# Hybrid decoder block on eight cores: norm factors in PSUM banks, a six-bank rotation and three changes to the planner's due times

## The chip, the cores and the metric

The kernel runs on the 8 cores of one Trainium2 chip as one program. Each core works on its own 2048 tokens (two sequences of 8192, four cores each) and nothing is exchanged between cores. The metric is the device time of one execution in microseconds, which is that of the slowest core. The profile is taken on the slowest core of one execution.

## The reference

```
for l in range(DEPTH):                                   # DEPTH = 1
    mod = (silu(c) @ w_ada[l] + b_ada[l])[:, None, :]
    sh1, sc1, ga1, sh2, sc2, ga2 = split(mod, 6)
    h = rms_norm(x, g_mix[l]) * (1 + sc1) + sh1
    z = h @ w_in[l] + b_in[l]
    q, k, v, conv_b, conv_c, conv_x, gate_a, gate_c = split(z, ...)
    attn = sliding_window_sink_attention(q, k, v, sinks[l])      # window 128
    conv = conv_b * causal_depthwise_conv(conv_c * conv_x, conv_w[l])   # 3 taps
    merged = sigmoid(gate_a) * attn + sigmoid(gate_c) * conv
    x = x + ga1 * (merged @ w_out[l])
    h = rms_norm(x, g_ffn[l]) * (1 + sc2) + sh2
    g_part, u_part = split(h @ w_ffn_in[l], 2)
    x = x + ga2 * ((silu(g_part) * u_part) @ w_ffn_out[l])
return rms_norm(x, g_final)
```

Width 1024, 16 query heads and 2 key heads of 64, feed-forward width 2816. All arrays are float32 in memory; the kernel multiplies in bfloat16.

## The kernel before

A core keeps its tokens in four tiles of 512, channels on the partitions. X (`xres`, float32) holds the residual, H (`h`, bfloat16) the normed input of either sub-layer, MG (`mg`) the merged branches and later the feed-forward activations.

Each operation is recorded with its engine, the intervals that it reads and writes, a cost in us, a priority and perhaps a `lat`. A planner (`schedule`, a list scheduler) then simulates the five engines with these costs: of the operations that are ready on an engine it takes the one with the lowest priority number, and an operation is ready when each of its inputs is done, plus `lat`. What it finds is a fixed order for each engine's queue. On the chip the engines follow these orders and wait only on semaphores. `lat` and the priorities thus put no wait into the program: they only place an instruction further back in its queue. `step_pos` counts the priority up by one for each piece of work.

The stages, in order:

1. Start and mixing (0 to about 510 us). Token-major tiles are squared and scaled (`prep`), turned by TensorE and evicted with shift and scale into H (`turned`, `turn`, L531 to L543). Then eight chunks of channels run: query, gate, convolution groups (`group`, L593), attention in nine steps (L721 to L773) and the merge on GpSimd (L784). The groups take PSUM banks 0 to 3 in rotation (`nb`), the scores banks 4 and 5, the attention sums banks 6 and 7. Between chunks 1 and 3, `mods_rows` makes the four late modulation vectors: a weight of 4 MB comes in over the GpSimd queue (`wadaB`), 16 matmuls in two halves (L791) give partial sums, ScalarE copies them out (L796), SyncE writes them to memory and reads them back transposed (L799, L802), and VectorE adds them up (L806, L809).
2. Output projection and the first feed-forward groups (about 504 to 605 us). `w_out` does eight groups of eight matmuls for each tile (L911), VectorE evicts them into X (L917), ScalarE squares (L896, L901) and GpSimd adds the squares into ACC (L903). `second_norm` follows for each tile: `rstd_of` sums ACC over partitions with one matmul (L470), ScalarE takes the root into RS (L473), VectorE the reciprocal into RS (L475), then eight products X times factor into H (L928, VectorE) and eight scale-and-shift instructions (L933, ScalarE). The tiles come in the order w0, w1, w2, f0, w3, f1, f2, f3, where f is the first four feed-forward steps (`ff_in`: two groups at L968, silu at L973, product at L976).
3. The rest of the feed-forward (605 to about 1036 us): three groups of hidden chunks, `ff_in` and `ff_out` (L981, evicted at L988).
4. `finish_tile`: the last norm in the same way, the products at L1004 on VectorE or L1009 on GpSimd, and the output transfers.

From stage 2 on, `nb` rotates over eight banks, in the order 4, 5, 6, 7, 0, 1, 2, 3, and `rstd_of` takes its bank from the same rotation. The bank of a group is fixed by the order in which the program records the groups. The bank of tile 2's sum (its root is the last reader) is therefore also that of the last group of f0.

Of the kernel before, what the change touches and what calls it, by code (L numbers as in the profile page):

```python
# [289 lines left out]
def build_program():  # L290
# [87 lines left out]
    with es:  # L378
# [86 lines left out]
        P.op("act", lambda e: e.activation(out=ESINK.t[:], in_=cst(O_SINK, 8), func=AF.Exp), reads=[cst_iv], writes=[ESINK.iv()], cost=1.5)  # L465


        def rstd_of(total, n, sd, slack=1.5):
            b = nb()
            P.op("pe", [lambda e: e.matmul(bank(b)[:, 0:n], lhsT=ONESF.t[:], rhs=total[0][total[1], total[1] + n], start=True, stop=True)],  # L470
                 reads=[ONESF.iv(), total[0].iv(total[1], total[1] + n)], writes=[pv_(b)], cost=4 * n / 2400 + 0.2, lat=slack)
            d, o = sd
            P.op("act", lambda e: e.activation(out=d[o, o + n], in_=bank(b)[:, 0:n], func=AF.Sqrt, bias=EPSC.t[:], scale=1.0 / D),  # L473
                 reads=[pv_(b), EPSC.iv()], writes=[d.iv(o, o + n)], cost=act_us(n))
            P.op("dve", lambda e: e.reciprocal(out=d[o + n, o + 2 * n], in_=d[o, o + n]),  # L475
                 reads=[d.iv(o, o + n)], writes=[d.iv(o + n, o + 2 * n)], cost=0.1 + n * 0.0066)

        def scaled(src, a, n, rs, hcol, eng):
            d, o = rs
            P.op(eng, lambda e: e.tensor_tensor(out=h3[:, :, hcol:hcol + n], in0=src[a, a + 8 * n].rearrange("p (k t) -> p k t", k=8),  # L480
                                                in1=d[o, o + n].rearrange("p (o t) -> p o t", o=1).to_broadcast([128, 8, n]), op=ALU.mult),
                 reads=[src.iv(a, a + 8 * n), d.iv(o, o + n)], writes=h_iv(hcol, n),
                 cost=dve_us(8 * n) if eng == "dve" else pool_us(8 * n))

        def affine(hcol, n, acol, shcol, ivs):
            for k in range(8):
                P.op("dve", lambda e, k=k: e.tensor_scalar(out=hk(k, hcol, n), in0=hk(k, hcol, n), scalar1=acol[:, k:k + 1],
                                                           scalar2=shcol[:, k:k + 1], op0=ALU.mult, op1=ALU.add),
                     reads=ivs + [H.iv(k * NTH + hcol, k * NTH + hcol + n)], writes=[H.iv(k * NTH + hcol, k * NTH + hcol + n)],
                     cost=dve_us(n, 4))  # L490


        def stats(src, a, nblk, s0, out, engs=("act",)):
# [56 lines left out]
            scale(X, tt * 4096, 4, 1 + 4 * tt, XN, ("dve",) * 4 if tt == 1 else ("dve", "act", "dve", "dve"))  # L550

        def turned(tt):
            turn(XN, 4, 128 + 512 * tt, None, ("dve",))

        stats(X, 0, 4, 1, XN0)
        stats(XH, 0, 1, 0, XNH)
# [231 lines left out]
        def mods_rows(slot, v):  # L788
            for hf in range(2):
                b = nb()  # L790
                P.op("pe", [lambda e, i=i, q=q, b=b, hf=hf: e.matmul(bank(b)[32 * q:32 * q + 32, :], lhsT=SCREP[(4 * i + q) * 32, (4 * i + q + 1) * 32],  # L791
                                                         rhs=WA[1][(4 * i + q) * 1024 + hf * 512, (4 * i + q) * 1024 + hf * 512 + 512],
                                                         start=(i == 0), stop=(i == 1), skip_group_check=True, tile_position=(0, 32 * q))
                            for i in range(2) for q in range(4)],
                     reads=[WA[1].iv(), SCREP.iv()], writes=[pv_(b)], cost=0.8)
                P.op("act", lambda e, hf=hf, b=b: e.activation(out=MROW[hf * 512, hf * 512 + 512], in_=bank(b), func=AF.Copy),  # L796
                     reads=[pv_(b)], writes=[MROW.iv(hf * 512, hf * 512 + 512)], cost=act_us(512, 0))
            dv = ("d", slot, slot + 1)
            P.op("sp", lambda e: e.dma_start(out=mscr_d[slot], in_=MROW.t[0:128:32, :]), reads=[MROW.iv()], writes=[dv],  # L799
                 dma="d_mr", cost=0.1, nbytes=16384)  # L800
            mo = slot * 32
            P.op("sp", lambda e: e.dma_start(out=MC4[mo, mo + 32].rearrange("p (q j) -> p q j", q=4),  # L802
                                             in_=mscr_d[slot].rearrange("q (j p) -> p q j", p=128),
                                             allow_slow_non_contiguous=True),
                 reads=[dv], writes=[MC4.iv(mo, mo + 32)], dma="d_mc", cost=0.1, nbytes=600000)
            P.op("dve", lambda e: e.tensor_reduce(out=MODC[v * 8, v * 8 + 8], in_=MC4[mo, mo + 32].rearrange("p (q j) -> p j q", q=4),  # L806
                                                  axis=AX.X, op=ALU.add),
                 reads=[MC4.iv(mo, mo + 32)], writes=[MODC.iv(v * 8, v * 8 + 8)], cost=0.2)
            P.op("dve", lambda e: e.tensor_tensor(out=MODC[v * 8, v * 8 + 8], in0=MODC[v * 8, v * 8 + 8], in1=cst(O_BADA + 8 * v, 8), op=ALU.add),  # L809
                 reads=[MODC.iv(v * 8, v * 8 + 8), cst_iv], writes=[MODC.iv(v * 8, v * 8 + 8)], cost=0.2)  # L810
            if v == 4:
                P.op("dve", lambda e: e.scalar_tensor_tensor(out=A2.t[:], in0=MODC[32, 40], scalar=1.0, in1=cst(O_GFFN, 8),
                                                             op0=ALU.add, op1=ALU.mult),
                     reads=[MODC.iv(32, 40), cst_iv], writes=[A2.iv()], cost=0.2)
# [106 lines left out]

        def second_norm(tt):
            ro = (tt % 2) * 1024
            rstd_of((ACC, (tt % 2) * 512), 512, (RS, ro))
            P.prio = pos[0] + 9
            for k in range(8):
                a = tt * 4096 + k * 512
                P.op("dve", lambda e, a=a, k=k: e.tensor_tensor(out=hk(k, 128 + 512 * tt, 512), in0=X[a, a + 512], in1=RS[ro + 512, ro + 1024], op=ALU.mult),  # L928
                     reads=[X.iv(a, a + 512), RS.iv(ro + 512, ro + 1024)], writes=[H.iv(k * NTH + 128 + 512 * tt, k * NTH + 640 + 512 * tt)],
                     cost=dve_us(512))  # L930
            for k in range(8):
                iv = H.iv(k * NTH + 128 + 512 * tt, k * NTH + 640 + 512 * tt)
                P.op("act", lambda e, k=k: e.activation(out=hk(k, 128 + 512 * tt, 512), in_=hk(k, 128 + 512 * tt, 512), func=AF.Identity,  # L933
# [258 lines left out]
```

How the kernel before makes its waits and increments, by code:

```python
    def replay(self, eng, engine, sems):  # L245
        for o in self.order[eng]:
            for s, v in self.waits[o.idx].items():
                engine.wait_ge(sems[s], v)
            ins = None
            for fn in o.fns:
                ins = fn(engine)
            if o.dma is not None:
                ins.then_inc(sems[o.dma], 16)
            elif o.need:
                ins.then_inc(sems[eng], 1)
# [847 lines left out]
        @block.sync  # L1103
        def _(eng):
            P.replay("sp", eng, sems)
            for i in range(8):
                eng.wait_ge(sems[f"d_o{i}"], P.dma_cnt[f"d_o{i}"])
```

## Time and profile before

| | us |
|---|---|
| median of 3 runs | 1089.92 |
| lowest and highest of them | 1057.12, 1121.12 |
| the profiled execution | 1056.61 |
| its span, slowest core (core 0) | 1054.5 |
| fastest core (core 3) | 1040.8 |
| TensorE busy on core 0 | 961.6 (91%) |
| VectorE busy | 585.1 (55%) |
| ScalarE, GpSimd busy | 385.6, 209.1 |

The execution's own time is 2.11 us above the span of its slowest core. A busy share says how long an engine had an instruction in it, not that it bounds the stage. Line numbers such as L968 are those of the kernel before; PE is TensorE, PEld its weight load, DVE VectorE, ACT ScalarE, POOL GpSimd, SP SyncE.

### The profile page before, as it was taken

The numbers are of one execution on the slowest core, as the hardware profiler recorded it, in microseconds if no ns is written. First come the engines' busy times: TensorE is split into PE (matmuls) and PEld (weight loads), VectorE is DVE, ScalarE is ACT, GpSimd is POOL, SyncE is SP. The second block draws the span as 40 slices with busy tenths as digits, with TensorE's granted clock in tenths as the row PEclk, the third lists the DMA queues.
The fourth block names the chain that finished last, engine by engine and source line by source line (L and its number), as shares of the span: only waits on it lengthen the run. The fifth ranks groups of instructions, "written<-read, shape, count | busy, mean of one in ns | idle before, by whom it ended". The sixth has DMA issues, their size and how long they took to land.

```text
span 1054.5 us, 15358 instructions; the slowest of 8 cores (1040.8 to 1054.5 us)
## 1 busy us (share of the span) xinstructions
PE 961.6 (91%) x5474; PEld 452.4 (43%) x5571; DVE 585.1 (55%) x829; ACT 385.6 (37%) x592; POOL 209.1 (20%) x282
## 2 busy tenths in 40 slices
PE   0469999999979999999998999999999999999993
PEld 0335444444434444444443444444444444444443
DVE  1247858586857877878868531234212244253656
ACT  4166545454535454545266531100111100233233
POOL 2100222222211212121563410000100001023213
PEclk9989999999989999999998999999999999999997
DMA  9970462855244434032800432210522202110222
GB/s 191 226 175 1 60 111 29 125 96 81 48 53 128 91 130 91 11 56 36 136 16 11 71 57 44 40 21 1 91 40 40 40 1 47 23 66 15 80 80 81
DMA packets 44651, 72.26 MB, mean 69 GB/s; under 512 B 19600, under 2 KB 21904, under 8 KB 42528
## 3 DMA queue, kind: packets, MB, share of 16 engines
q0 software_dynamic: 21600, 45.36, 27.1%
q1 hardware_dynamic: 22976, 25.91, 8.1%
q8 instruction: 46, 0.75, 0.3%
q14 instruction: 29, 0.24, 0.1%
HBM read 108.15 MB, written 8.45 MB: 111 GB/s over the span
## 4 chain that ended last, share of the span: by engine, by line
PE 78%; DVE 8%; DMA 6%; issue 4%; ACT 2%; POOL 1%; DVEq 0%; ACTq 0%; POOLq 0%; SPq 0%
PE psum L968 28%; PE psum L593 27%; PE psum L981 14%; DMA wadaB<-w_ada_l 5%; PE psum L911 3%; PE psum L745 3%; DVE rden L770 2%; PE psum L721 2%; DMA mc<-mscr 1%; DVE h L928 1%; DVE h L543 1%; DVE cv L668 1%; DVE nrm L771 1%; DVE pT L733 1%; PE psum L531 0%
## 5 line engine op out<-in xcount | busy, mean ns | idle before, releaser
L593 PE MATMUL psum<-h,ws 128*128 128x512 bf16 (+1 forms) x1694 | 366.0, 366 | 15.7 <-issue 5.7
L968 PE MATMUL psum<-h,fws 128*128 128x512 bf16 x1380 | 306.1, 380 | 6.0 <-ACT rs L473 4.5
L593 PEld LDWEIGHTS psum<-h,ws 128*128 128x128 bf16 x1744 | 161.4, 99 | 188.6 <-issue 38.6
L968 PEld LDWEIGHTS psum<-h,fws 128*128 128x128 bf16 x1408 | 138.0, 98 | 173.3 <-issue 9.4
L976 DVE TENSOR_TENSOR mg<-psum,sg 128x512 bf16<-128x512 f32 x88 | 60.4, 688 | 196.5 <-PE psum L968 189.6
L973 ACT ACTIVATE sg<-psum 128x512 bf16<-128x512 f32 x88 | 52.1, 596 | 307.6 <-PE psum L968 297.6
L981 PE MATMUL psum<-mg,fwo 128*128 128x512 bf16 (+1 forms) x747 | 152.4, 363 | 1.7 <-DVE mg L976 1.0
L770 DVE RECIPROCAL rden<-rden 128x256 f32<-128x256 f32 x64 | 111.9, 1749 | 12.6 <-ACT rden L768 11.6
L988 DVE SCALAR_TENSOR_TENSOR xres<-psum,modc,xres 128x512 f32<-128x512 f32 (+1 forms) x104 | 73.7, 709 | 78.3 <-PE psum L981 77.5
L981 PEld LDWEIGHTS psum<-mg,fwo 128*128 128x128 bf16 x760 | 74.3, 98 | 79.2 <-issue 1.5
L784 POOL TENSOR_TENSOR mg<-nrm,cv 128x256 bf16<-128x256 f32 x64 | 53.8, 840 | 273.8 <-DVE cv L690 141.4
L903 POOL TENSOR_TENSOR acc<-acc,sq 128x512 f32<-128x512 f32 (+1 forms) x58 | 69.7, 1203 | 126.0 <-ACT sq L901 120.6
L730 ACT ACTIVATE pT<-psum 128x1024 bf16<-128x1024 f32 (+2 forms) x72 | 66.7, 926 | 52.8 <-PE psum L721 52.8
L911 PE MATMUL psum<-mg,ws 128*128 128x512 bf16 x250 | 57.5, 383 | 3.5 <-ACT rs L473 1.3
L955 POOL DMA_DIRECT2D fws<-w_fi_l x44 | 23.5, 536 | 170.3 <-PE psum L968 155.7
L733 DVE TENSOR_TENSOR pT<-pT,mask 128x1024 bf16<-128x1024 bf16 (+2 forms) x72 | 45.8, 640 | 12.1 <-ACT pT L730 11.5
L668 DVE SCALAR_TENSOR_TENSOR cv<-u,cst,cv 128x512 f32<-128x512 f32 x64 | 48.0, 749 | 7.6 <-ACT cv L665 4.9
L901 ACT ACTIVATE sq<-xres 128x512 f32<-128x512 f32 (+1 forms) x63 | 36.2, 581 | 41.9 <-DVE xres L988 21.3
L768 ACT ACTIVATE rden<-psum,esink 128x256 f32<-128x256 f32 x64 | 29.7, 470 | 47.5 <-PE psum L745 47.3
L656 DVE SCALAR_TENSOR_TENSOR u<-psum,cst,cx 128x410 f32<-128x410 f32 x40 | 25.6, 640 | 37.2 <-PE psum L593 33.6
L442 POOL DMA_DIRECT2D ws<-w_in_l x50 | 27.6, 560 | 90.9 <-DMA xres<-xtok 40.5
L745 PE MATMUL psum<-pT,vS 128*64 128x128 bf16 (+1 forms) x384 | 37.0, 248 | 6.1 <-DVE nrm L771 4.5
(89 smaller groups left out, 679.1 us busy)
## 6 DMA issues: line engine op xcount, KB each, us to landing
ws<-w_in_l POOLq DMA_DIRECT2D x50, 256.0 KB, 5.7
fws<-w_fi_l POOLq DMA_DIRECT2D x44, 256.0 KB, 4.7
wadaB<-w_ada_l POOLq DMA_DIRECT2D x20, 512.0 KB, 6.8
xres<-xtok SPq DMA_DIRECT2D x8, 1024.0 KB, 11.8
xres<-xt SPq DMA_DIRECT2D x8, 1024.0 KB, 6.0
out<-xres SPq DMA_DIRECT2D x12, 512.0 KB, 2.6
fwo<-w_fo_l POOLq DMA_DIRECT2D x22, 256.0 KB, 5.0
wadaA<-w_ada_l POOLq DMA_DIRECT2D x4, 512.0 KB, 19.2
```

The lines of the kernel that those rows point to most:

```text
L593: P.op("pe", [lambda e, k=k: e.matmul(bank(b)[:, 0:n], lhsT=WS[s * 1024 + k * 128, s * 1024 + (k + 1) * 128], rhs=hk(k, col, n), start=(k ...
L668: P.op("dve", lambda e, tap=tap: e.scalar_tensor_tensor(out=CV[a, a + 512], in0=U[a + tap, a + tap + 512], scalar=cst(O_CONV + 8 * tap + c ...
L730: P.op("act", lambda e: e.activation(out=p3[:, :, c0:c1], in_=sc2[:, :, c0:c1], func=AF.Exp, scale=0.125), reads=[pv_(4, 2)], writes=[PT.i ...
L733: P.op("dve", lambda e: e.tensor_tensor(out=p3[:, :, c0:c1], in0=p3[:, :, c0:c1], in1=m0.rearrange("p (o q) -> p o q", o=1).to_broadcast([ ...
L745: out.append(lambda e, hd=hd, r0=r0, lhs=lhs, den=den: e.matmul(bank(bk)[r0:r0 + 64, den + c0:den + c0 + w], lhsT=lhs, rhs=PT[o + hd * 512 ...
L770: P.op("dve", lambda e: e.reciprocal(out=rd, in_=rd), reads=[riv], writes=[riv], cost=1.75)
L903: P.op(addeng, lambda e: e.tensor_tensor(out=ACC[acc, acc + n], in0=ACC[acc, acc + n], in1=SQ[o, o + n], op=ALU.add), reads=[ACC.iv(acc, a ...
L911: P.op("pe", [lambda e, c=c: e.matmul(bank(b), lhsT=WS[s * 1024 + c * 128, s * 1024 + (c + 1) * 128], rhs=MG[c * 2048 + tt * 512, c * 2048 ...
L968: P.op("pe", [lambda e, k=k, w=w, wo=wo, b=b: e.matmul(bank(b), lhsT=w[wo + k * 128, wo + (k + 1) * 128], rhs=hk(k, 128 + tt * 512, 512), ...
L976: P.op("dve", lambda e: e.tensor_tensor(out=MG[m0, m0 + 512], in0=bank(bs[1]), in1=SG[o, o + 512], op=ALU.mult), reads=[pv_(bs[1]), SG.iv( ...
L981: P.op("pe", [lambda e, jl=jl: e.matmul(bank(b)[:, 0:n], lhsT=FO[jl * 1024 + co * 128, jl * 1024 + (co + 1) * 128], rhs=MG[jl * 2048 + tt ...
L988: P.op("dve", lambda e: e.scalar_tensor_tensor(out=X[a0, a1], in0=bank(b)[:, 0:n], scalar=MODC[40 + co, 41 + co], in1=X[a0, a1], op0=ALU.m ...
```

## The change

Four things, and the planner then makes a new order for the whole program. (1) The matmuls of `mods_rows` get `lat=5.0` and a cost of 1.05 in place of 0.8, and the first VectorE sum gets `lat=25.0`. (2) `rstd_of` takes a fixed bank, 6 or 7 by the tile's parity; for the second norm and for the last norm of whole tiles (and the last half tile) the reciprocal is written into that bank, and the products read it from there in place of RS. From stage 2 on the rotation is over the six banks 0 to 5. (3) Tile 1's four turned banks are evicted by VectorE and ScalarE in turn, not by VectorE alone. (4) The second norm's products of tiles 1 and 2 are ranked 16 positions on, not 9. Two unused functions go.

```
-        def rstd_of(total, n, sd, slack=1.5):
-            b = nb()
+        def rstd_of(total, n, sd, slack, b, in_psum):
...
-            P.op("dve", lambda e: e.reciprocal(out=d[o + n, o + 2 * n], in_=d[o, o + n]),
-                 reads=[d.iv(o, o + n)], writes=[d.iv(o + n, o + 2 * n)], cost=0.1 + n * 0.0066)
...
+            P.op("dve", lambda e: e.reciprocal(out=bank(b)[:, 0:n] if in_psum else d[o + n, o + 2 * n], in_=d[o, o + n]),
+                 reads=[d.iv(o, o + n)], writes=[pv_(b)] if in_psum else [d.iv(o + n, o + 2 * n)], cost=0.1 + n * 0.0066)
...
-            turn(XN, 4, 128 + 512 * tt, None, ("dve",))
+            turn(XN, 4, 128 + 512 * tt, None, ("dve", "act") if tt == 1 else ("dve",))
...
-                     reads=[WA[1].iv(), SCREP.iv()], writes=[pv_(b)], cost=0.8)
+                     reads=[WA[1].iv(), SCREP.iv()], writes=[pv_(b)], cost=1.05, lat=5.0)
...
-                 reads=[MC4.iv(mo, mo + 32)], writes=[MODC.iv(v * 8, v * 8 + 8)], cost=0.2)
+                 reads=[MC4.iv(mo, mo + 32)], writes=[MODC.iv(v * 8, v * 8 + 8)], cost=0.2, lat=25.0)
...
-            rstd_of((ACC, (tt % 2) * 512), 512, (RS, ro))
-            P.prio = pos[0] + 9
+            sb = 6 + tt % 2
+            rstd_of((ACC, (tt % 2) * 512), 512, (RS, ro), 1.5, sb, True)
+            P.prio = pos[0] + (16 if tt in (1, 2) else 9)
...
-                P.op("dve", lambda e, a=a, k=k: e.tensor_tensor(out=hk(k, 128 + 512 * tt, 512), in0=X[a, a + 512], in1=RS[ro + 512, ro + 1024], op=ALU.mult),
+                P.op("dve", lambda e, a=a, k=k: e.tensor_tensor(out=hk(k, 128 + 512 * tt, 512), in0=X[a, a + 512], in1=bank(sb), op=ALU.mult),
...
+            sb = 6 + i % 2
+            on_bank = len(on_dve) == 8 or n == 512
+            rstd_of((ACC, (i % 2) * 512), n, (RS, ro), 1.5 if n == 512 else 0.0, sb, on_bank)
...
-                rs = RS[ro + n, ro + 2 * n]
+                rs = bank(sb)[:, 0:n] if on_bank else RS[ro + n, ro + 2 * n]
...
-        banks[:] = [4, 5, 6, 7, 0, 1, 2, 3]
+        banks[:] = [0, 1, 2, 3, 4, 5]
```

## Rows read from the trace of the kernel before

**Rows 1.** The page's head and its busy time of each engine.
```profile
span 1054.5 us, 15358 instructions; the slowest of 8 cores (1040.8 to 1054.5 us)
...
PE 961.6 (91%) x5474; PEld 452.4 (43%) x5571; DVE 585.1 (55%) x829; ACT 385.6 (37%) x592; POOL 209.1 (20%) x282
```

**Rows 2.** Spans and mean granted TensorE clock, three of the cores.
```profile
core 0: 1054.5 us, clock 0.984
...
core 6: 1046.8 us, clock 0.979
core 7: 1054.4 us, clock 0.979
```

**Rows 3.** TensorE's waits, core 0: us in total, times, longest us.
```profile
PE psum L745 <- DVE nrm L771: 4.5, 2, 4.3
PE psum L968 <- ACT rs L473: 4.5, 2, 4.0
...
PE psum L791 <- DMA wadaB<-w_ada_l: 2.4, 2, 1.8
...
PE psum L593 <- DVE h L543: 1.5, 1, 1.5
PE psum L911 <- ACT rs L473: 1.3, 2, 0.8
PE psum L911 <- ACT pT L730: 1.3, 1, 1.3
```

**Rows 4.** Stretches, core 0: length, PE, PEld, DVE, ACT, POOL busy; PEclk, DMA share, GB/s.
```profile
300.00:320.00 20.00, 17.71 (x83) 8.12 (x85) 11.39 (x15) 6.92 (x11) 3.31 (x5) 0.83 0.28 74
...
570.00:605.00 35.00, 31.63 (x131) 13.76 (x134) 19.79 (x24) 19.67 (x28) 12.57 (x14) 0.90 0.39 61
605.00:840.00 235.00, 233.84 (x1069) 106.52 (x1090) 65.97 (x94) 36.56 (x60) 19.02 (x36) 1.00 0.26 40
```

**Rows 5.** Timeline, core 0, 275 to 312 us: start, us, instruction, idle before.
```profile
287.18 0.36 SPq L802 DMA_DIRECT2D mc<-mscr  x1
...
294.00 0.25 PE L745 MATMUL psum<-pT,vS 128*64 128x128 bf16 x2 [0.43 <-DVE pT L733]
...
299.30 0.20 DVE L806 TENSOR_REDUCE modc<-mc 128x8 f32<-128x32 f32 x1 [5.25 <-DMA mc<-mscr]
...
302.21 0.32 PE L745 MATMUL psum<-pT,vS 128*64 128x128 bf16 x2 [4.35 <-DVE nrm L771]
```

**Rows 6.** Timeline of TensorE, core 6: the same two points.
```profile
293.57 0.25 PE L745 MATMUL psum<-pT,vS 128*64 128x128 bf16 x2 [0.43 <-DVE pT L733]
...
565.17 3.57 PE L968 MATMUL psum<-h,fws 128*128 128x512 bf16 x8 [4.00 <-ACT rs L473]
```

**Rows 7.** Timelines of DVE, ACT and PE, core 0, 512 to 610 us.
```profile
558.65 9.12 DVE L928 TENSOR_TENSOR h<-xres,rs 128x512 bf16<-128x512 f32 x8
...
572.63 3.35 DVE L475 RECIPROCAL rs<-rs 128x512 f32<-128x512 f32 x1 [1.60 <-ACT rs L473]
...
577.07 4.89 DVE L928 TENSOR_TENSOR h<-xres,rs 128x512 bf16<-128x512 f32 x8
...
547.16 4.34 ACT L933 ACTIVATE h<-h,modc,a 128x512 bf16<-128x512 bf16 x6 [0.76 <-DVE h L928]
...
553.94 12.25 PE L968 MATMUL psum<-h,fws 128*128 128x512 bf16 x55
...
572.78 3.57 PE L968 MATMUL psum<-h,fws 128*128 128x512 bf16 x8 [4.00 <-ACT rs L473]
```

**Rows 8.** One line's instructions: ns min/median/max, first and last start, forms.
```profile
L928 DVE TENSOR_TENSOR h<-xres,rs x32: 677/681/1756, 543.8 to 610.7; 128x512 bf16<-128x512 f32 x32
...
L976 DVE TENSOR_TENSOR mg<-psum,sg x88: 626/692/693, 567.7 to 1023.5; 128x512 bf16<-128x512 f32 x88
```

**Rows 9.** Timeline of VectorE, core 0, tile 1's first six evictions.
```profile
68.98 2.80 DVE L543 TENSOR_SCALAR h<-psum,a,modc 128x512 bf16<-128x512 bf16 x6 [3.69 <-PE psum L531]
```

More of the change, by code:

```diff
@@ L474, in rstd_of @@
                  reads=[pv_(b), EPSC.iv()], writes=[d.iv(o, o + n)], cost=act_us(n))
-            P.op("dve", lambda e: e.reciprocal(out=d[o + n, o + 2 * n], in_=d[o, o + n]),
-                 reads=[d.iv(o, o + n)], writes=[d.iv(o + n, o + 2 * n)], cost=0.1 + n * 0.0066)
[L478 to L490, printed above, removed]
+            P.op("dve", lambda e: e.reciprocal(out=bank(b)[:, 0:n] if in_psum else d[o + n, o + 2 * n], in_=d[o, o + n]),
+                 reads=[d.iv(o, o + n)], writes=[pv_(b)] if in_psum else [d.iv(o + n, o + 2 * n)], cost=0.1 + n * 0.0066)
         def stats(src, a, nblk, s0, out, engs=("act",)):
@@ L923, in second_norm @@
             ro = (tt % 2) * 1024
-            rstd_of((ACC, (tt % 2) * 512), 512, (RS, ro))
-            P.prio = pos[0] + 9
+            sb = 6 + tt % 2
+            rstd_of((ACC, (tt % 2) * 512), 512, (RS, ro), 1.5, sb, True)
+            P.prio = pos[0] + (16 if tt in (1, 2) else 9)
             for k in range(8):
                 a = tt * 4096 + k * 512
-                P.op("dve", lambda e, a=a, k=k: e.tensor_tensor(out=hk(k, 128 + 512 * tt, 512), in0=X[a, a + 512], in1=RS[ro + 512, ro + 1024], op=ALU.mult),
-                     reads=[X.iv(a, a + 512), RS.iv(ro + 512, ro + 1024)], writes=[H.iv(k * NTH + 128 + 512 * tt, k * NTH + 640 + 512 * tt)],
-                     cost=dve_us(512))
+                P.op("dve", lambda e, a=a, k=k: e.tensor_tensor(out=hk(k, 128 + 512 * tt, 512), in0=X[a, a + 512], in1=bank(sb), op=ALU.mult),
+                     reads=[X.iv(a, a + 512), pv_(sb)], writes=[H.iv(k * NTH + 128 + 512 * tt, k * NTH + 640 + 512 * tt)],
+                     cost=dve_us(512, 1, True))
             for k in range(8):
@@ L996, in finish_tile @@
             P.prio = pos[0] + (5 if n == 512 else 0)
-            rstd_of((ACC, (i % 2) * 512), n, (RS, ro), 1.5 if n == 512 else 0.0)
+            sb = 6 + i % 2
+            on_bank = len(on_dve) == 8 or n == 512
+            rstd_of((ACC, (i % 2) * 512), n, (RS, ro), 1.5 if n == 512 else 0.0, sb, on_bank)
             P.prio = pos[0] + (14 if n == 512 else 1)
@@ L1000, in finish_tile @@
                 a0, a1 = xi(tt, co, lo, n)
-                rs = RS[ro + n, ro + 2 * n]
-                io = dict(reads=[X.iv(a0, a1), RS.iv(ro + n, ro + 2 * n), cst_iv], writes=[X.iv(a0, a1)])
+                rs = bank(sb)[:, 0:n] if on_bank else RS[ro + n, ro + 2 * n]
+                io = dict(reads=[X.iv(a0, a1), pv_(sb) if on_bank else RS.iv(ro + n, ro + 2 * n), cst_iv], writes=[X.iv(a0, a1)])
                 if n == 512 or co in on_dve:
```

## The prediction

> **What bounds the kernel.** I read the page first: TensorE is busy 961.6 of 1054.5 us, VectorE 585.1 [rows 1]. TensorE is thus the bound in most places, and the change can give back only time in which TensorE stands still, or runs at its lower clock. So the next view is TensorE's waits, and the one after it the stretches, which say where waiting is left. Two waits of the list can be touched by this change and are long: 4.3 us for the attention product L771 and 4.0 us for the root L473; four smaller ones come to 6.5 us: 2.4 for the modulation weights, 1.5 for tile 1's evictions, 1.3 and 1.3 at L911 [rows 3]. From 605 us on there is nothing to win: TensorE is busy 233.84 of 235 us [rows 4]. Last, the cores: 0 and 7 end at 1054.5 and 1054.4 us, core 6 at 1046.8 [rows 2], the fastest at 1040.8 [rows 1]. The metric is the slowest, so a stall that only some cores have is worth the distance to the next core, no more.
>
> **Late modulation sums.** On core 0 the read-back of the sums was issued at 287.18 us and VectorE stood before L806 for 5.25 us, until 299.30; everything behind it in VectorE's queue came late, among it L771, for which TensorE then waited 4.35 us, until 302.21 [rows 5]. TensorE's granted clock was 0.83 of full in 300 to 320 us [rows 4]: it fell to the half level after that idle time, so the stall costs more than its own length. The cost can be read from two cores. From the attention matmul before the stall to the feed-forward matmul at L968 core 0 took 572.78 - 294.00 = 278.78 us [rows 5, 7], core 6, without the stall, 565.17 - 293.57 = 271.60 [rows 6]. The stall costs 7.2 us. With the sum planned 25 us after the transfer's end it stands behind VectorE work that takes longer than the 12 us from 287.18 to 299.30, so the wait is gone. Nobody asks for the vector soon: the nearest user is L917, in stage 2. What is late next is core 6, which ends at 1046.8 us [rows 2] and has no such stall: the gain of the slowest core is 1054.5 - 1046.8 = 7.7 us, in which a few tenths come from the matmul wait below.
>
> **Modulation matmuls.** Their `lat` of 5 us moves 8 halves of 8 matmuls back on TensorE, past the wait for the weights, 2.4 us in two waits on core 0 [rows 3]. Moved with them are the copies L796, the write and the read-back on SyncE's queue (nothing else is due there), and the release of the weight buffer, on which the next load on GpSimd's queue waits; behind that stand merges and weight loads. The cost is not shown in the trace. Below: a gain of 2.4 us, already in the step to core 6 for the most part. Above: `lat` also counts from the release of the bank, one of four in rotation, so the fourth group behind may find it just being copied; a wait on a bank in this trace is at most 1.3 us [rows 3], four times that is 5 us. I take +1 us, since the other engines' orders have slack in this stage.
>
> **The bank of the sum.** Before, the last group of f0 shares the bank of tile 2's sum. TensorE stood 4.00 us until 572.78 for that root, and the eight matmuls that followed took 3.57 us. Seven such groups from 553.94 took 12.25 us, 1.75 each (one record of 56 is missing), hence another 1.8 us at the lower clock [rows 7]; the stretch from 570 shows a mean clock of 0.90 [rows 4]. The root no longer holds a bank of the rotation, so 4.0 + 1.8 = 5.8 us go, on core 6 as well, which has the same row [rows 6]. What is late next: with six banks this group waits for the bank of f0's first pair, that is for L976 on VectorE. In the trace that product stood behind eight products of tile 1 that took 9.12 us from 558.65 [rows 7]; the later rank lets it pass in front. That is why I take 5.8 and not less; if the product stays behind, 2 to 3 us come back.
>
> **The small waits at L911.** The two for the root and the one for the scores' banks are 2.6 us [rows 3]; with banks 0 to 3 first they go, or are replaced by a wait for the last convolution evictions. Behind them f0 needs tile 0's normed input, whose last scale ends near 551.5 us while TensorE comes to f0 at 553.94 [rows 7]: 2.4 us of slack, so a gain above that would be lost to this chain. I take 1.5 us, bounds 0 and 2.6.
>
> **The factor in PSUM.** 32 products of the second norm and 32 of the last norm read PSUM. The nearest row is L976, also a 128x512 product with one operand in PSUM: 692 ns median against 681 for L928 [rows 8]; 32 times 11 ns is 0.35 us on an engine with room. Against that, eight products took 4.89 us where GpSimd was not adding and 9.12 where it was [rows 7], with single ones up to 1756 ns, while L976 never exceeds 693 over 88 [rows 8]. So tile 1's eight should fall to 5.0 to 5.6 us. This is off TensorE's path except through the chain above; worth 0 to 1 us there, and I count it in the 1.5.
>
> The Trainium skill speaks for this part and against it. "SBUF — State Buffer", section "SBUF: two separate sides", says that a VectorE instruction with two SBUF inputs and a GpSimd instruction that reads SBUF lock each other out for a whole instruction; the trace's 9.12 against 4.89 us agrees, and by it the products are freed too. "VectorE: DVE Perf Modes", section "The TRN2 errata", gives a PSUM source 62 cycles more than an SBUF source at 0.96 GHz, an estimate of 65 ns, or 2.1 us over 32 products instead of 0.35; the trace's 11 ns doesn't bear it out, and VectorE's room would hide either.
>
> **Tile 1's evictions.** VectorE took 2.80 us for six of eight [rows 9], and TensorE waited 1.5 us behind the last two [rows 3]. That pair goes to ScalarE now, at about the same length, so only the pairs ahead, and the convolution product behind them, come earlier. I take 0.3 us, bounds -0.5 and 1.5.
>
> **Sum.** 7.7 + 5.8 + 1.5 + 0.3 - 1.0 = 14.3 us; the tail (reciprocal and eight half products) keeps its lengths. Span 1054.5 - 14.3 = 1040.2, with 2.1 around it 1042.3, against the profiled 1056.61: 1.4% less. The median of the three runs lies 33.3 us above that execution, the lowest, 1057.12, beside it; my sum is made against the latter.
>
> **Rivals.** (A) Only the modulation stall goes, and the bank wait is replaced by one for L976 and by the chain of tile 0's norm: 7.7 + 3 - 1 = 9.7 us, 1047. For it: VectorE was 9.12 us in one set of products while f0 ran [rows 7]. Against: the new rank. Chance 0.2. (B) The new order pays more: all small waits go (2.6 + 1.5 + 2.4) and no new one comes: 7.7 + 5.8 + 6.5 = 20 us, and with a start like core 3's 1 to 3 more, 1034 to 1037. Just here the 2% line lies, at 1035.5. Chance 0.2. (C) Slower: six banks are too few. A group takes 1.75 us, so with five ahead VectorE may be away for 8.7 us. A reciprocal of 3.35 and eight products at 9.12 [rows 7], if the planner sets them in one piece and GpSimd still blocks them, are 12.5 us: 3.8 us of stall and 1.8 at the lower clock, for each of four second norms 22 us, so 1042 + 22 = 1065. It decides once a burst passes 8.7 us; free of GpSimd it is 3.35 + 4.89 = 8.2, near it. Against: the evictions are ranked ahead of the products. Chance 0.08. (D) The order doesn't do what it says, the sum at L806 still meets its transfer: 1050. The 25 us are twice the 12 from 287.18 to 299.30 [rows 5], so 0.04. My forecast keeps 0.48.
>
> **Range and chances.** Forecast and A and B span 1034 to 1047. A median of a few runs may stand where the three runs shown had theirs, 33.3 us above the profiled execution; less the 14.3 that is 1075.6. The range to hold 8 in 10 is therefore 1034 to 1076; without that offset it would be 1034 to 1052. Two per cent is about what a measurement of this kernel can tell from no change. Faster by over 2%: the lower part of B and part of the offset, 0.22; within: 0.69; slower: 0.09, that is C and its like.
>
> **What would show it.** Right: no VectorE wait before the sum at L806 on any core and clock 1.00 in 300 to 320 us; cores 0 and 7 no longer 8 us behind; no TensorE wait for the root L473; tile 1's products at some 0.69 us each. Wrong: TensorE waits in 540 to 605 us for L976, L917 or L933, or for a bank near 240 and 280 us; or a new first wait in the start, which sets the order of the cores.

## The result and the profile after

The changed kernel's runs lie at 1045.05 to 1046.46 us, the kernel before at 1056.95 and 1057.12; the ratio is 0.9895, 95% interval 0.9866 to 0.9923, that is 1.1% or some 11 us less. In a second measurement it was 0.9891 (0.9864 to 0.9917). Left aside are one run of the changed kernel at 1228.46, in which four cores had a mean clock of only 0.81 to 0.82, and two slow ones of before, 1089.92 and 1121.12, with which the median of before would be 1073.52. The forecast was 1042.3 against 1056.61, 14.3 us less; the profiled execution of after took 1045.05.

The cores of after, first the spans:

```profile
core 0: 1041.9 us, clock 0.980
core 1: 1042.2 us, clock 0.981
...
core 3: 1043.2 us, clock 0.980
...
core 6: 1041.6 us, clock 0.980
core 7: 1042.4 us, clock 0.981
```

They stand within 1.6 us of each other, where those of before were 13.7 us apart [rows 1, 2]; in the changed kernel's other runs here the distance was 4.5 and 3.8 us. The stall of core 0 behind the read-back [rows 5] is gone. This is the line of the sum (L792 in the numbers of after) on core 3, and then the stretch from 300 to 320 us on cores 0 and 3, to be read beside [rows 4]:

```profile
L792 DVE TENSOR_REDUCE modc<-mc x4: 127/200/201, 200.7 to 324.8; 128x8 f32<-128x32 f32 x4
its engine sat idle before it (us, times) until:
who waited for it (us, times):
  POOL mg L770: 17.3, 2
```

```profile
300.00:320.00 20.00, 19.79 (x120) 9.41 (x120) 10.56 (x16) 8.15 (x13) 2.60 (x4) 1.00 0.60 134
...
300.00:320.00 20.00, 20.00 (x111) 9.45 (x110) 10.46 (x17) 8.31 (x13) 2.60 (x4) 1.00 0.67 148
```

Nothing stands under "sat idle before it", on this core as on the other seven: VectorE no longer waits for the transfer, and the clock is 1.00 where it was 0.83. GpSimd's merges (L770) now stand behind the later sum, but no TensorE wait for a merge is in TensorE's list. In that list of waits on core 3 the root is gone too, and something else has come, which answers to the second line of [rows 3]:

```profile
PE psum L579 <- DMA ws<-w_in_l: 5.3, 1, 5.3
...
PE psum L897 <- DVE xres L903: 3.3, 2, 3.0
...
PE psum L731 <- DVE nrm L757: 2.3, 3, 1.2
...
PE psum L579 <- ACT mrow L782: 1.2, 2, 0.7
```

The 5.3 us are in the start; on cores 1, 4, 5 and 7 of before the same wait was 4.3 to 5.1 us. The 3.0 us are new, and stand on all eight cores. The timelines of TensorE and VectorE around them, core 3:

```profile
540.05 3.77 PE L897 MATMUL psum<-mg,ws 128*128 128x512 bf16 x16
546.85 3.49 PE L897 MATMUL psum<-mg,ws 128*128 128x512 bf16 x8 [3.03 <-DVE xres L903]
...
532.40 3.36 DVE L475 RECIPROCAL psum<-rs 128x512 f32<-128x512 f32 x1 [3.40 <-ACT rs L473]
535.67 0.67 DVE L903 SCALAR_TENSOR_TENSOR xres<-psum,ga,xres 128x512 f32<-128x512 f32 x1
536.26 4.86 DVE L915 TENSOR_TENSOR h<-xres,psum 128x512 bf16<-128x512 f32 x8
541.04 0.74 DVE L903 SCALAR_TENSOR_TENSOR xres<-psum,ga,xres 128x512 f32<-128x512 f32 x1
542.75 3.36 DVE L475 RECIPROCAL psum<-rs 128x512 f32<-128x512 f32 x1 [0.97 <-ACT rs L473]
546.02 3.96 DVE L903 SCALAR_TENSOR_TENSOR xres<-psum,ga,xres 128x512 f32<-128x512 f32 x6
```

From 532.40 to 546.02, 13.6 us, VectorE evicts only two banks (L903, the L917 of before): a reciprocal, eight products, another reciprocal. A group of eight matmuls takes 1.75 us, so six banks last TensorE for some 10.5 us. The group that starts at 546.85 needs the bank that the first of the six evictions from 546.02 sets free. TensorE stands 3.03 us, and the eight matmuls behind take 3.49 us in place of 1.75: a price of 4.8 us, where the root's wait of before cost 5.8 (4.00 and 3.57, [rows 7]).

**A ladder of stretches.** Each is read on every core from the first and last starts of three lines: the group matmuls, the output projection and `ff_out` (L593, L911, L981 before; L579, L897, L968 after). What is called the projection stretch runs from the first output-projection matmul to the first `ff_out` matmul, so the first feed-forward groups lie in it. For core 0 of before they are these rows:

```profile
L593 PE MATMUL psum<-h,ws x1694: 219/379/634, 47.5 to 508.2; 128*128 128x512 bf16 x116, 128*128 128x410 bf16 x71, 128*128 128x128 bf16 x2
...
L911 PE MATMUL psum<-mg,ws x250: 376/379/631, 505.0 to 589.0; 128*128 128x512 bf16 x125
...
L981 PE MATMUL psum<-mg,fwo x747: 269/379/379, 687.4 to 1036.5; 128*128 128x512 bf16 x159, 128*128 128x256 bf16 x28
```

The start is 47.5; mixing, up to the first output-projection matmul, 505.0 - 47.5 = 457.5; the projection stretch 687.4 - 505.0 = 182.4; the feed-forward 349.1; the tail 1054.5 - 1036.5 = 18.0. The feed-forward stretch was 349.1 or 349.2 on every core of every kernel below, the tail 17.7 to 18.4, so the table keeps the other two.

| kernel | start | mixing | projection stretch | slowest core |
|---|---|---|---|---|
| before | 44.2 to 47.5 | 448.2 to 459.3 | 181.1 to 182.8 | 1054.5 |
| changed | 45.8 to 47.6 | 448.9 to 450.5 | 179.3 to 179.5 | 1043.2 |
| delays alone | 44.6 to 48.3 | 450.6 to 451.8 | 183.0 to 187.7 | 1052.9 |
| the sum's delay alone | 44.2 to 48.1 | 449.0 to 451.3 | 181.3 to 186.6 | 1052.0 |
| banks alone | 44.9 to 47.8 | 446.2 to 458.2 | 179.1 to 179.3 | 1051.5 |
| changed, no delays | 44.3 to 47.8 | 446.5 to 461.1 | 177.9 to 180.4 | 1055.1 |
| changed, factor in SBUF | 44.9 to 48.2 | 448.6 to 449.9 | 179.3 | 1043.6 |
| changed, rank 9 | 44.1 to 48.3 | 447.9 to 450.4 | 179.2 to 180.1 | 1044.9 |
| changed, matmuls' delay off | 46.0 to 48.4 | 446.5 to 450.1 | 177.5 to 179.3 | 1043.0 |
| changed, seven banks | 44.6 to 47.7 | 448.0 to 450.2 | 174.0 to 174.3 | 1038.3 |
| seven banks, matmuls' delay off | 44.3 to 48.2 | 447.2 to 449.4 | 174.0 to 177.0 | 1039.9 |
| seven banks, VectorE turns alone | 45.3 to 48.0 | 448.6 to 450.4 | 174.0 to 174.8 | 1039.3 |
| eight banks, sums recorded late | 44.9 to 48.0 | 447.2 to 449.4 | 177.9 to 179.7 | 1043.7 |

### The profile page after: what moved, and what is told of

It reads as the page before. It is cut to its first block, busy times and chain, and to the rows that moved or that the text cites. A ratio compares the mean times of both kernels' runs of the same rounds, so it can differ in the third digit from the quotient of the medians.

```text
span 1043.1 us, 15483 instructions; the slowest of 8 cores (1041.6 to 1043.2 us)
## 1 busy us (share of the span) xinstructions
PE 967.1 (93%) x5571; PEld 450.4 (43%) x5571; DVE 579.2 (56%) x825; ACT 388.3 (37%) x596; POOL 207.8 (20%) x282
## 4 chain that ended last, share of the span: by engine, by line
PE 79%; DVE 10%; DMA 4%; issue 3%; ACT 2%; POOL 1%; DVEq 0%; ACTq 0%; POOLq 0%
PE psum L955 29%; PE psum L579 27%; PE psum L968 14%; DVE rden L756 4%; PE psum L897 4%; DMA ws<-w_in_l 4%; PE psum L731 2%; PE psum L707 1%; DVE cv L654 1%; DVE nrm L757 1%; DVE pT L719 1%; DVE cv L662 1%; PE psum L470 1%; DVE u L642 1%; PE psum L517 1%
## 5 line engine op out<-in xcount | busy, mean ns | idle before, releaser
L579 PE MATMUL psum<-h,ws 128*128 128x512 bf16 (+1 forms) x1744 | 373.1, 366 | 9.4 <-DMA ws<-w_in_l 4.5
L955 PE MATMUL psum<-h,fws 128*128 128x512 bf16 x1408 | 306.3, 379 | 0.0
L579 PEld LDWEIGHTS psum<-h,ws 128*128 128x128 bf16 x1744 | 160.7, 98 | 187.8 <-issue 37.2
L955 PEld LDWEIGHTS psum<-h,fws 128*128 128x128 bf16 x1408 | 138.0, 98 | 168.4 <-issue 4.0
L968 PE MATMUL psum<-mg,fwo 128*128 128x512 bf16 (+1 forms) x760 | 153.1, 363 | 1.0 <-DVE mg L963 1.0
L968 PEld LDWEIGHTS psum<-mg,fwo 128*128 128x128 bf16 x760 | 74.3, 98 | 79.2 <-issue 1.5
L770 POOL TENSOR_TENSOR mg<-nrm,cv 128x256 bf16<-128x256 f32 x64 | 53.7, 839 | 262.8 <-DVE cv L676 123.5
L716 ACT ACTIVATE pT<-psum 128x1024 bf16<-128x1024 f32 (+2 forms) x72 | 66.7, 927 | 45.3 <-PE psum L707 45.3
L897 PE MATMUL psum<-mg,ws 128*128 128x512 bf16 x256 | 58.3, 385 | 4.0 <-DVE xres L903 3.3
L654 DVE SCALAR_TENSOR_TENSOR cv<-u,cst,cv 128x512 f32<-128x512 f32 x64 | 48.3, 755 | 6.7 <-ACT cv L651 3.9
L897 PEld LDWEIGHTS psum<-mg,ws 128*128 128x128 bf16 x256 | 24.7, 99 | 35.9 <-issue 8.3
```

The lines of the kernel that those rows point to most:

```text
L579: P.op("pe", [lambda e, k=k: e.matmul(bank(b)[:, 0:n], lhsT=WS[s * 1024 + k * 128, s * 1024 + (k + 1) * 128], rhs=hk(k, col, n), start=(k ...
L654: P.op("dve", lambda e, tap=tap: e.scalar_tensor_tensor(out=CV[a, a + 512], in0=U[a + tap, a + tap + 512], scalar=cst(O_CONV + 8 * tap + c ...
L716: P.op("act", lambda e: e.activation(out=p3[:, :, c0:c1], in_=sc2[:, :, c0:c1], func=AF.Exp, scale=0.125), reads=[pv_(4, 2)], writes=[PT.i ...
L770: P.op("pool", lambda e: e.tensor_tensor(out=MG[m0, m0 + 256], in0=NR[no, no + 256], in1=CV[a, a + 256], op=ALU.add), reads=[NR.iv(no, no ...
L897: P.op("pe", [lambda e, c=c: e.matmul(bank(b), lhsT=WS[s * 1024 + c * 128, s * 1024 + (c + 1) * 128], rhs=MG[c * 2048 + tt * 512, c * 2048 ...
L955: P.op("pe", [lambda e, k=k, w=w, wo=wo, b=b: e.matmul(bank(b), lhsT=w[wo + k * 128, wo + (k + 1) * 128], rhs=hk(k, 128 + tt * 512, 512), ...
```

## The experiments

Where no ratio is given, one execution was measured. The changed kernel's own runs lie between 1044.69 and 1046.46 us, so a difference of a microsecond between two such times says nothing; the stretches of the table say more.

**The delays alone.** The kernel before with

```
-                     reads=[WA[1].iv(), SCREP.iv()], writes=[pv_(b)], cost=0.8)
+                     reads=[WA[1].iv(), SCREP.iv()], writes=[pv_(b)], cost=1.05, lat=5.0)
...
-                 reads=[MC4.iv(mo, mo + 32)], writes=[MODC.iv(v * 8, v * 8 + 8)], cost=0.2)
+                 reads=[MC4.iv(mo, mo + 32)], writes=[MODC.iv(v * 8, v * 8 + 8)], cost=0.2, lat=25.0)
```

> The kernel before with the two planning delays alone (5 us at the modulation matmuls, 25 us at the sum); banks, evictions and ranks as before. Theory: these two lines are most of the gain, because they bring all cores to the pace of those that had no stall. From the first group matmul to the first output-projection matmul every core takes 449 to 451 us (before: 448.2 to 449.8 without the stall, 454 to 459 with it), the stretch from there to the first ff_out matmul stays at 181 to 183 us, the slowest core ends at 1045 to 1047 us, ratio 0.990 to 0.993. Rival: the banks are most of the gain; then the slowest core stays above 1049.

Measured: ratio 0.9972 (0.9955 to 0.9990), slowest core 1052.9. The mixing stretch came out as expected but for 1 us: no core is left with a stall. The time did not: the projection stretch grew to 183 to 187.7 us, and more than half of the gain went there, in two ways. On core 6 TensorE's timeline has a wait that neither before nor after has:

```profile
510.63 6.78 PE L911 MATMUL psum<-mg,ws 128*128 128x512 bf16 x24 [3.13 <-DMA ws<-w_out_l]
```

A projection weight issued at 503.31 us isn't there when its group's turn comes, and the 24 matmuls behind took 6.78 us in place of some 5.3, at a clock of 0.83 in 510 to 520 us. In the new order a group comes up before its weight. That isn't all: on core 7 no wait for a weight over 0.15 us is found, and its stretch is 183.0 against 181.5 before. There the clock fell although TensorE had had no wait over 0.15 us since 565.23 us; core 7 here, and the same core before, with the columns of [rows 4]:

```profile
580.00:590.00 10.00, 10.00 (x42) 4.22 (x40) 2.15 (x4) 4.79 (x7) 8.64 (x8) 0.85 0.21 35
...
580.00:590.00 10.00, 10.00 (x48) 4.50 (x47) 7.87 (x13) 7.00 (x12) 4.78 (x8) 1.00 0.78 123
```

In 580 to 590 us the mean granted clock was 0.83 to 0.86 on all eight cores of this run and 1.00 on all eight of before. In every run with the six-bank rotation, delays or not, factor in SBUF or not, old ranks or not, the stretch is 177.5 to 180.4 us, so the cure goes with the rotation. Why this order asks for the weight earlier, and why the clock falls here, stays open.

**The sum's delay alone.** The second of the two edits, without the first.

> The kernel before with the 25 us at the sum alone, the modulation matmuls without their delay. Theory: the stall is the read-back that the sum waits for, so this line alone removes the 4 to 5 us wait of TensorE for the attention product, and the waits for the modulation weights (2.4 us on the cores that start late) stay. Mixing stretch 448 to 451 us on every core, slowest core 1044 to 1048. Rival: the matmuls' delay is needed too; then one or more cores keep a stretch above 453.

Measured: one profile, 1053.96 us, slowest core 1052.0. The mixing stretch is 449.0 to 451.3 us on all cores, so this line alone removes the stall, and the rival is out. The weight's wait is there as well (1.99 us on core 7, whose projection stretch is 186.6), and so is the lower clock in 580 to 590 us, 0.81 to 0.88 on six of the eight cores; the total missed in the same way.

**The banks alone.** The kernel before with `rstd_of` on bank 6 or 7 and

```
-        banks[:] = [4, 5, 6, 7, 0, 1, 2, 3]
+        banks[:] = [0, 1, 2, 3, 4, 5]
```

factor in RS, ranks, evictions and delays as before.

> The kernel before with the roots' sums on banks 6 and 7 and a rotation over the other six from the output projection on; the factor stays in SBUF, ranks and evictions as before, no planning delays. Theory: the root's wait (4.0 us at the last group of f0) goes, and six banks give a new wait behind a reciprocal and a burst of products, of 3 us or more, since here GpSimd still blocks the products; the stretch from the first output-projection matmul to the first ff_out matmul is 180 to 186 us, so no gain to speak of. Rival, the forecast's own: 5.8 us go and the stretch is 176 us. The slowest core keeps its stall in the mixing stage if the read-back lands late, 1047 to 1058.

Measured: ratio 0.9952 (0.9928 to 0.9975). The projection stretch is 179.1 to 179.3 us on every core, 1.8 to 3.7 us less than before against the forecast's 7.3, as in the changed kernel. TensorE's timeline on core 3:

```profile
518.40 1.89 PE L897 MATMUL psum<-mg,ws 128*128 128x512 bf16 x8 [0.76 <-DVE cv L662]
...
551.24 3.61 PE L897 MATMUL psum<-mg,ws 128*128 128x512 bf16 x16 [1.27 <-DVE xres L903]
556.70 12.25 PE L955 MATMUL psum<-h,fws 128*128 128x512 bf16 x56 [1.85 <-DVE xres L903]
...
583.47 3.61 PE L897 MATMUL psum<-mg,ws 128*128 128x512 bf16 x16 [1.18 <-DVE xres L903]
```

The root's wait has been replaced by four waits for evictions, 5.1 us in all, and the groups behind them kept 1.75 to 1.9 us each. The one of 3 us or more that I expected isn't among them. Cores 3, 5 and 6 have the stall of the mixing stage, 455.5 to 458.2 us.

**The changed kernel without the delays.** Both undone.

> The changed kernel with the two planning delays taken back. Theory: the stretch from the first output-projection matmul to the first ff_out matmul keeps the 179.4 us of the changed kernel, and the mixing stretch goes back to 448 to 459 us with the cores apart by 8 to 10 us; slowest core 1050 to 1054, ratio 0.996 to 0.999. Rival: banks and evictions are the gain, and the slowest core is at 1043.

Measured: ratio 0.9976 (0.9950 to 1.0002), slowest core 1055.1, a microsecond outside. Core 0, VectorE and TensorE:

```profile
304.87 0.20 DVE L792 TENSOR_REDUCE modc<-mc 128x8 f32<-128x32 f32 x1 [7.06 <-DMA mc<-mscr]
```

```profile
307.78 0.32 PE L731 MATMUL psum<-pT,vS 128*64 128x128 bf16 x2 [6.17 <-DVE nrm L757]
```

The stall is back and longer, and core 3 of the same execution, without it, ends at 1037.5. So the two parts don't add: alone they gave 0.28% and 0.24% (the latter not clear of no change), together 1.05%. Without the delays the slowest core keeps its stall whatever the banks save; without the banks the projection stretch gives most of the delays' gain back, by the late weight and the lower clock above.

**The factor in SBUF.** The changed kernel with RS as the products' second input and the reciprocal's output.

> The changed kernel with the norm factor kept in SBUF again; its six-bank rotation, ranks and delays stay. Theory: the PSUM factor is off TensorE's path. The products of tile 1 take longer where GpSimd adds (8 of them 6 to 9 us in place of 5.0), the stretch from the first output-projection matmul to the first ff_out matmul stays within 0.5 us of 179.4. Rival (the skill's lock, on the path): the evictions come later behind the blocked products, the wait for a bank grows from 3.0 to 5 us and the stretch to 182.

Measured: 1045.39 us, projection stretch 179.3 on every core. On VectorE the factor in PSUM did what was forecast. Eight products of tile 0 (4.86 us in the changed kernel, above) and the eight of tile 1 took here, on core 3:

```profile
535.16 5.97 DVE L915 TENSOR_TENSOR h<-xres,rs 128x512 bf16<-128x512 f32 x8
...
552.71 5.58 DVE L915 TENSOR_TENSOR h<-xres,rs 128x512 bf16<-128x512 f32 x4
...
558.81 2.48 DVE L915 TENSOR_TENSOR h<-xres,rs 128x512 bf16<-128x512 f32 x4
```

Tile 1's are 8.1 us; in the changed kernel they took 1.28, 1.87 and 1.87 in three pieces, 5.0 us, where the forecast had 5.0 to 5.6. The 32 products of the changed kernel (compare [rows 8], with its maximum of 1756):

```profile
L915 DVE TENSOR_TENSOR h<-xres,psum x32: 674/680/682, 536.3 to 597.5; 128x512 bf16<-128x512 f32 x32
```

None is blocked any more, and none is dearer: 680 ns with the factor in PSUM; with it in SBUF 681 on core 0 of before and 682 on core 3 here. In the total it is worth nothing, but that is a balance. With the factor in SBUF the order is another, with three evictions between the two reciprocals and not two: TensorE's waits in this stretch on core 3 are 5.5 us against 4.2 in the changed kernel (1.09 and 1.85 for evictions, 1.38 of the sum L470 for GpSimd's adds), but the clock stayed at 1.00 on every core, where the changed kernel lost some 1.7 us by it.

**The rank.** The changed kernel with all ranks 9.

> The changed kernel with all second-norm products ranked 9 positions on, as before. Theory: the rank decides nothing for the sum of the waits: the one long wait of 3.0 us is split into shorter ones for the same engine, as in the run with the banks alone, stretch 178.5 to 180 us. Rival, the forecast's reason for its full 5.8 us: without the rank the last group of f0 waits behind the products, 2 to 3 us more, stretch 182.

Measured: 1046.86 us, projection stretch 179.2 to 180.1. The long wait stayed one wait, 3.02 us at the same place, against my guess that it would be split; no stretch of 182. The 180.1 are cores 6 and 7, whose clock was 0.98 and 0.95 in 570 to 590 us as well. The rank is worth nothing either, and the splitting in the runs with the banks alone or the factor in SBUF (1.09 and 1.85 us on core 3) goes with the factor's place.

**Seven banks.** The changed kernel with

```
-            sb = 6 + tt % 2
+            sb = 7
...
-            sb = 6 + i % 2
+            sb = 7
...
-        banks[:] = [0, 1, 2, 3, 4, 5]
+        banks[:] = [0, 1, 2, 3, 4, 5, 6]
```

> The changed kernel with one bank for all roots' sums (7) and a rotation over seven. Theory: the rotation of six is the cause of the 3.0 us wait for an output-projection eviction behind a reciprocal; one bank more is one group more, 1.7 us, so the wait falls below 1.5 us, the clock stays up behind it, and the stretch from the first output-projection matmul to the first ff_out matmul falls from 179.4 to 175.5 to 177.5 us. Rival: VectorE is late by its own load, whatever the banks; the stretch stays at 179 or more.

Measured: 1040.31 us, projection stretch 174.0 to 174.3 on every core, better than either of my numbers. TensorE and VectorE on core 3:

```profile
526.53 13.98 PE L897 MATMUL psum<-mg,ws 128*128 128x512 bf16 x64
540.34 1.02 PE L470 MATMUL psum<-acc,onesf 128*128 128x512 f32 x2
541.20 1.89 PE L897 MATMUL psum<-mg,ws 128*128 128x512 bf16 x8
542.93 13.98 PE L955 MATMUL psum<-h,fws 128*128 128x512 bf16 x64
```

```profile
534.34 4.86 DVE L915 TENSOR_TENSOR h<-xres,psum 128x512 bf16<-128x512 f32 x8
539.12 4.04 DVE L903 SCALAR_TENSOR_TENSOR xres<-psum,ga,xres 128x512 f32<-128x512 f32 x6
543.61 3.36 DVE L475 RECIPROCAL psum<-rs 128x512 f32<-128x512 f32 x1 [0.46 <-ACT rs L473]
```

No bracket stands behind any of these matmuls: TensorE doesn't wait, and on no core is there a wait over 0.8 us in this stretch. Two things have changed. There is a bank more, and since tile 1's sum now needs the bank that tile 0's products read, its reciprocal comes after six evictions and not before them. The run doesn't separate the two. The starts of the groups and the ends of the evictions in the two traces allow an estimate: with the changed kernel's order of evictions a seventh bank would leave 1.3 us of wait (a feed-forward group due near 545.4, its bank free at 546.70), and with this run's order six banks would leave 1.2 us (a group at 538.62, its bank free at 539.86), of 3.3 us in all. So neither does it alone.

**The modulation matmuls' delay.** The changed kernel without the 5 us (cost 0.8), and then the same with seven banks.

> The changed kernel with the modulation matmuls placed as before (no 5 us, cost 0.8); the 25 us at the sum stay. Theory: the waits for the copy out of a shared bank (1.2 us in two) go, and those for the weights come back on cores that start late (1 to 2.5 us): mixing stretch 448 to 451 us against 448.9 to 450.5, slowest core within 1.5 us of the changed kernel's. Rival: the 5 us are needed against the stall; then some core has a stretch above 453.

> The changed kernel with one bank for all roots' sums, a rotation over seven, and the modulation matmuls placed as before (the 25 us at the sum stay). Theory: the two gains of the runs before add up: stretch from the first output-projection to the first ff_out matmul 174.0 us, mixing 447 to 450, slowest core 1034 to 1038, ratio 0.980 to 0.984. Rival: with the matmuls undelayed the earlier arrival at the output projection meets a weight that lands late (seen with the delays alone), stretch 176 or more on some cores, ratio 0.985.

Measured: the first 1044.85 us, mixing 446.5 to 450.1; the second, ratio 0.9847 (0.9822 to 0.9872), mixing 447.2 to 449.4. The median of the eight cores is 448.3 in place of 449.35 with six banks and 448.25 in place of 449.05 with seven. The wait behind L782, 1.2 us in the changed kernel, isn't in either. So the 5 us cost about 1 us, and no core had a mixing stretch above 453: they aren't needed. The second run's slowest core, 1039.9, and ratio came out a little above what I expected: its cores 2 and 3 took 176.7 and 177.0 us in the projection stretch. The rival's late weight is there, but small: 0.89 us on core 5 (stretch 175.0), 0.23 on core 3, none over 0.15 on core 2. What cost cores 2 and 3 their time is in the last section.

**Tile 1's evictions.** Seven banks, and `("dve",)` for tile 1 again.

> The changed kernel with seven banks in rotation and tile 1's turned banks evicted by VectorE alone, as before. Theory: the shared eviction is worth nothing that can be seen (forecast 0.3 us): mixing stretch 448 to 450.5 us, as with seven banks alone (448.0 to 450.2), TensorE's wait before tile 1's first group 1.5 us in place of 1.7 to 1.9. Rival: it is worth 1 us or more, mixing 449.5 to 451.5.

Measured: 1041.18 us, mixing 448.6 to 450.4 against 448.0 to 450.2. On core 3 the two waits around tile 1's evictions are 1.33 and 1.25 us with VectorE alone, 0.91 and 1.69 with ScalarE's help in the changed kernel: 2.58 against 2.60. The share moves the wait and doesn't shorten it.

**Eight banks, sums recorded late.** No fixed bank; the norms of tiles 1 to 3 recorded one to three steps later, priorities kept, factor in SBUF, the matmuls' delay off:

```
-        for what, tt in (("w", 0), ("w", 1), ("w", 2), ("f", 0), ("w", 3), ("f", 1), ("f", 2), ("f", 3)):
+        for what, tt in (("w", 0), ("w", 1), ("n", 0), ("w", 2), ("f", 0), ("n", 1), ("w", 3), ("n", 2), ("f", 1), ("n", 3), ("f", 2), ("f", 3)):
```

> Another way out of the same collision: all eight banks stay in rotation and the roots take theirs from it, but tile 1's, 2's and 3's second norm is recorded only one to three steps later (after f0, w3, f1), so that no feed-forward group shares a bank with a root that is still to come; factor in SBUF, priorities of the changed kernel, 25 us at the sum, no 5 us. Theory: it is the sharing of a bank by order of recording that costs, so the stretch from the first output-projection to the first ff_out matmul is 173.5 to 176 us and the slowest core ends at 1034 to 1039. Rival: fixed banks are needed, since a root's bank in the rotation blocks a group somewhere; the stretch is 178 or more.

Measured: ratio 0.9891 (0.9864 to 0.9917), projection stretch 177.9 to 179.7. The rival was right, but for another object. Core 3:

```profile
586.71 1.10 PE L470 MATMUL psum<-acc,onesf 128*128 128x512 f32 x2 [2.55 <-ACT sg L960]
```

Now it is tile 3's sum that shares its bank with a feed-forward group, by the order of recording the first of f1, eight places earlier in the rotation. TensorE has the sum in its queue ahead of f1's last groups and stands until ScalarE has done that group's silu. Moving the record moves the collision. The two other things undone here, the factor and the 5 us, don't explain the 177.9 to 179.7: alone they left 179.3 and 177.5 to 179.3.

**The changed kernel again.**

> The changed kernel once more, beside the others on this chip. Both theories: slowest core 1041 to 1045, ratio 0.987 to 0.992, stretch from the first output-projection to the first ff_out matmul 179.4 us.

Measured: 0.9891 (0.9864 to 0.9917), slowest core 1043.7, projection stretch 179.2 to 179.5.

## Why the prediction was right or wrong

On the two profiled executions the change is 1054.5 - 1043.2 = 11.3 us, forecast 14.3. By the ladder, core 0 before against core 3 after: start 0.3, mixing 457.5 - 449.7 = 7.8, projection stretch 182.4 - 179.4 = 3.0, tail 0.2. (The wait of 1.26 us for the scores' bank stands right before the first output-projection matmul, so the ladder counts it to mixing.) The forecast had 7.7 + 0.3 - 1.0 = 7.0 for the start and mixing and 5.8 + 1.5 = 7.3 for the projection stretch.

- **The late sums: right, in mechanism, place and size.** The stall went from every core and the cores came together. 7.0 against 8.1 with the start, or 6.8 without the scores' wait. The 25 us alone do it: no core of the run with them alone took more than 451.3 us.
- **The modulation matmuls, +1.0: right.** The price is a wait for a bank being copied out, twice, 1.2 us (L579 behind L782, at 247.66 and 291.15 us), and the two runs without the delay give 0.8 and 1.05 us. The upper bound for it rested on a misreading: [rows 3] has waits on a bank longer than 1.3 us, 1.5 for tile 1's evictions and 4.0 for the root.
- **The bank of the sum, 5.8: this step failed.** The root's wait did go. The text asked what is late next, and looked in the wrong place: it named the feed-forward product L976, expected to be let pass by the new rank, and therefore took the full 5.8. What came was an eviction of the output projection (L917), ahead of f0, behind two reciprocals and eight products: 3.0 us of wait and 1.75 at the lower clock, so that of the 5.8 us only 1.0 was left. The text's own signs of being wrong had named it: a wait for L917 in 540 to 605 us. This is the mechanism of rival C, six banks too few; I had given it a chance of 0.08 because I priced it at all four norms or none (22 us), where one burst in four was enough for 4.8. The row that I needed was there: my own limit of 8.7 us without eviction against 3.35 + 4.89 + 3.35 for the reciprocals of two neighbouring tiles around one set of products, 11.6. I counted one reciprocal. With seven banks the stretch is 174.0 to 174.3, that is 6.8 to 8.8 us below the 181.1 to 182.8 of before: about the 7.3 of the forecast was there to be had in this stage, and the changed kernel reached less than half of it.
- **The small waits at L911, 1.5: right, within their bounds.** Those for the roots (1.3) and for the scores' bank (1.26) are gone, and 0.76 us for the last convolution eviction came, as the text had as an alternative: 1.8 us net. A further one of 0.55 for L771, which the text didn't count, went too, and 0.24 for an eviction came. The scores' wait still stands in the run with the delays alone, which has the old bank order, and its mixing stretch is longer by 1.7 us in the median of the cores (451.05 against 449.35).
- **The factor in PSUM: right on the engine; that it is off the path isn't shown.** The total is the same with the factor in SBUF, but by a balance of other waits against the clock. The estimate from the figures of the Trainium skill, "VectorE: DVE Perf Modes", section "The TRN2 errata", 65 ns more for a PSUM source, isn't borne out: 680 against 681 ns. The lock that the Trainium skill describes in "SBUF — State Buffer", section "SBUF: two separate sides", agrees with the trace: with the factor in PSUM the longest product fell from 1756 to 682 ns.
- **The rank: wrong as a reason.** It was to let the product L976 pass; with rank 9 the stretch is the same on six cores, and TensorE has no wait for that product over 0.15 us on core 3.
- **Tile 1's evictions, 0.3: nothing to be seen**, within its bounds.
- **The range.** Its lower part was sound; its upper end came from the offset between the median and the profiled execution, not from a cause in the kernel. Against the profiled execution the forecast was 1.4% less, and the ratio came out at 1.05% less. Set against the first median, 1089.92, the same 1042.3 reads as 4.4% less, which the sum never claimed: the forecast should have been given as a ratio to the profiled execution.

## What to carry to other kernels

When a wait on a bank is removed by taking banks out of a rotation, add up the longest time in which the evicting engine evicts nothing, over neighbouring tiles with every long instruction in it and the few evictions between them, and hold it against the banks that are left times one group's time. A stall of one core is worth the distance to the next core, and two repairs in different stages can be worth more together than alone, since the slowest core needs both (here 1.05% against 0.28% and 0.24%). A product freed from a lock and a step ranked later gained nothing here, on an engine that is busy for 55% of the time. When two kernels take the same time, compare their waits and their clock before calling a part worthless. Ask of a planned delay whether it stands before the transfer's user, where it is free, or also in a queue that shares buffers, where it costs.

## What the runs showed of the hardware

The lower clock doesn't follow a wait of a given length every time. The wait of 3.02 to 3.03 us for L903 stands on all cores of the changed kernel, of the run without the matmuls' delay (2.3 us on its core 7) and of the run without both delays. Behind it the mean clock fell on all eight cores of the first, on five of the second and on seven of the third. The second's core 0, then its core 3:

```profile
546.57 2.37 PE L897 MATMUL psum<-mg,ws 128*128 128x512 bf16 x8 [3.02 <-DVE xres L903]
548.74 11.55 PE L955 MATMUL psum<-h,fws 128*128 128x512 bf16 x47
...
545.28 1.89 PE L897 MATMUL psum<-mg,ws 128*128 128x512 bf16 x8 [3.02 <-DVE xres L903]
547.00 10.52 PE L955 MATMUL psum<-h,fws 128*128 128x512 bf16 x48
```

On core 3 nothing is slower. On core 0 the clock fell later, in part behind the group, in the matmuls at L955, and the price is the usual one: its projection stretch is 179.2 us, that of cores 1, 3 and 6, where the clock stayed up, 177.5 to 177.6. So some 1.7 us of such a wait's price is a matter of the core and the execution.

It can also fall with no wait of TensorE in front, as in the run with the delays alone. In the run with seven banks and no matmuls' delay core 3 was busy throughout this time, and yet:

```profile
572.78 10.68 PE L955 MATMUL psum<-h,fws 128*128 128x512 bf16 x40
583.28 1.23 PE L470 MATMUL psum<-acc,onesf 128*128 128x512 f32 x2
```

```profile
570.00:580.00 10.00, 10.00 (x42) 0.85 0.16 23
580.00:590.00 10.00, 10.00 (x40) 0.86 0.61 88
```

(the columns of the stretches: length, TensorE busy with its matmuls, granted clock, DMA share, GB/s). The same 40 matmuls took 8.80 us on core 3 of the run with seven banks, at a clock of 1.00. That is 1.9 of the 3.0 us by which this core's projection stretch, 177.0, stands above 174.0. Core 2, at 176.7, has 0.86 in both of these stretches; the other six cores have 1.00. In two more runs it was again two neighbouring cores at once: 6 and 7 with rank 9 (0.98 and 0.95), 4 and 5 with VectorE's turns alone (0.92 in 570 to 580 us, projection stretch 174.8 against 174.0 on the other six). With the delays alone it was all eight. What made the clock fall stays open.
